# Attention scores in paired PSUM banks: row groups alternating, one mask product per bank

## The reference

```python
for l in range(DEPTH):                      # 2
    x = x + 0.5 * swiglu(rmsnorm(x), ...)   # D_FF = 2816
    c_q, c_kv, k_pe, q_s, k_s, v_s = split(rmsnorm(x) @ w_in[l])
    # latent group: 4 heads, 128 columns without and 64 with rotary, dense causal
    out_a = dense_causal_attention(q_a, k_a, v_a, MLA_QK ** -0.5)
    # window group: 8 heads of 64 over 2 key/value heads, window 128, a sink per head
    out_b = sliding_window_sink_attention(q_b, k_b, v_b, swa_sinks[l], SWA_HEAD_DIM ** -0.5)
    x = x + concat(rmsnorm(out_a), rmsnorm(out_b)) @ w_o[l]
    x = x + 0.5 * swiglu(rmsnorm(x), ...)
```

## Time and profile before

| | us |
|---|---|
| median of 3 runs | 1009.09 |
| lowest, highest | 1000.56, 1010.95 |
| span of the profiled execution, first to last instruction | 999.5 |
| own time of the profiled execution, taken as the run nearest above its span | 1000.56 |
| PE busy in it | 966.5 |
| DVE busy | 565.5 |
| ACT busy | 473.6 |
| attention of the first layer, block 0's scores to the fifth output chunk | 243.2 to 290.8 |

### The profile page before, as it was taken

The page is one execution under the profiler, slowest core; times in us unless marked ns, Lnnn a source line. Parts: engine busy times, 40 slices in busy tenths (PEclk is TensorE's granted clock), DMA queues, the critical chain, the costliest instruction groups (busy, mean ns, idle before and its releaser), DMA issues.

```text
span 999.5 us, 13783 instructions
## 1 busy us (share of the span) xinstructions
PE 966.5 (97%) x4504; PEld 773.4 (77%) x4504; DVE 565.5 (57%) x763; ACT 473.6 (47%) x831; POOL 53.0 (5%) x85
## 2 busy tenths in 40 slices
PE   5999999999899999999989999999998999999998
PEld 4888878888677878788768788887876777878876
DVE  4654545486766644545465454545877665454544
ACT  5543434464656544444355343435456654443433
POOL 2000000022110000000010000000220100000000
PEclk9999999999999999999989999999999999999999
DMA  8765554560044764646357555463501466464641
GB/s 296 248 198 181 174 203 155 182 212 21 22 158 142 232 226 132 227 146 212 124 184 230 192 170 208 153 222 129 190 1 59 156 206 230 138 222 147 208 170 43
DMA packets 46251, 168.61 MB, mean 169 GB/s; under 512 B 5216, under 2 KB 5216, under 8 KB 46208
## 3 DMA queue, kind: packets, MB, share of 16 engines
q1 hardware_dynamic: 44496, 162.02, 48.1%
q0 software_dynamic: 1568, 5.52, 1.8%
q10 hardware_dynamic: 144, 0.52, 0.1%
HBM read 167.00 MB, written 1.05 MB: 168 GB/s over the span
## 4 chain that ended last, share of the span: by engine, by line
issue 75%; PE 17%; POOL 5%; DMA 1%; DVE 1%; ACT 0%; POOLq 0%; DVEq 0%; ACTq 0%; SPq 0%
PE UV L919 3%; PE UV L917 3%; PE UV L918 3%; PE A L917 2%; PE A L918 2%; PE A L919 2%; POOL rs_x L307 1%; DMA raw<-stream 1%; POOL rs_s L307 1%; POOL rs_x L305 1%; POOL rs_m L307 1%; DVE xn L634 1%; POOL gain L285 0%; PE UV L961 0%; ACT whi L367 0%
## 5 line engine op out<-in xcount | busy, mean ns | idle before, releaser
L612 DVE TENSOR_TENSOR wlo<-raw,whi 128x1024 fp32r<-128x1024 f32 x306 | 361.8, 1222 | 113.2 <-ACT whi L367 112.9
L367 ACT ACTIVATE whi<-raw 128x1024 fp32r<-128x1024 f32 x306 | 308.0, 1053 | 114.7 <-DMA raw<-stream 113.8
L917 PE MATMUL UV<-whi,act_hi 128*128 128x512 f32 (+1 forms) x752 | 299.6, 398 | 4.1 <-issue 3.4
L919 PE MATMUL UV<-whi,act_lo 128*128 128x512 f32 (+1 forms) x752 | 292.2, 389 | 0.0
L918 PE MATMUL UV<-wlo,act_hi 128*128 128x512 f32 (+1 forms) x752 | 290.8, 387 | 0.0
L917 PEld LDWEIGHTS UV<-whi,act_hi 128*128 128x128 f32 x752 | 142.6, 190 | 32.7 <-issue 3.9
L919 PEld LDWEIGHTS UV<-whi,act_lo 128*128 128x128 f32 x752 | 142.3, 189 | 30.5
L918 PEld LDWEIGHTS UV<-wlo,act_hi 128*128 128x128 f32 x752 | 142.9, 190 | 27.3
L655 DVE TENSOR_TENSOR ht_lo<-UV,ht_hi 128x256 fp32r<-128x256 f32 x88 | 37.1, 422 | 213.4 <-ACT ht_hi L403 213.4
L403 ACT ACTIVATE ht_hi<-UV 128x256 fp32r<-128x256 f32 x88 | 33.2, 378 | 236.6 <-PE UV L961 236.6
L917 PE MATMUL A<-whi,ht_hi 128*128 128x512 f32 x352 | 141.7, 402 | 0.5 <-DVE ht_lo L655 0.4
(11 more groups left out here) (131 smaller groups left out, 655.3 us busy)
## 6 DMA issues: line engine op xcount, KB each, us to landing
raw<-stream SPq DMA_DIRECT2D x306, 512.0 KB, 4.4
gain<-norm_gains POOLq DMA_DIRECT2D x9, 512.0 KB, 5.7
out<-x SPq DMA_DIRECT2D x2, 512.0 KB, 2.6
sgain<-small_gains POOLq DMA_DIRECT2D x2, 324.0 KB, 5.0
x<-x_in SPq DMA_DIRECT2D x1, 512.0 KB, 3.4
x<-x_in ACTq DMA_DIRECT2D x1, 512.0 KB, 8.2
cs<-rope POOLq DMA_DIRECT2D x1, 128.0 KB, 6.0
cgain<-col_gains POOLq DMA_DIRECT2D x2, 1.0 KB, 5.5
```

The lines of the kernel that those rows point to most:

```text
L367: act.activation(whi_half(unit, half), raw[:, n % RAW, :], ACT.Copy).then_inc(hi_done, 1)
L612: dve.tensor_tensor(wlo_half(unit, half), raw[:, n % RAW, :], whi_half(unit, half).bitcast(F32), ALU.subtract).then_inc(split_done, 1)
L917: pe.matmul(dst, hi, w_hi, start=start, stop=False, skip_group_check=True)
L919: return pe.matmul(dst, lo, w_hi, start=False, stop=stop, skip_group_check=True)
```

## The change

The order of the window heads in `BANKS` changes, so that each even bank holds heads of the first key/value head (rows 0 to 63) and the next bank the matching heads of the second (rows 64 to 127). `scores` is gone. `latent_scores` forms both latent banks in one go: all four 128-row products, then the four 64-row products with the row group alternating from one to the next, then one mask product of two heads (256 columns) for each bank. `window_scores` forms two window banks in one go: one mask product of 512 columns for each, which starts the bank, then the heads' products with banks and row groups alternating. It waits for the exponentials of both banks before it. PE's order around them is rewritten by pairs. The orders of DVE, ACT, GpSimd and SP are as before.

```diff
         def score_banks(t):
             per = 4 // (t + 1)
-            return [(True, [0, 2]), (True, [1, 3])] + [(False, list(range(i, i + per))) for i in range(0, SH, per)]
+            swa = [(False, list(range(kv * 4 + i, kv * 4 + i + per))) for i in range(0, 4, per) for kv in range(SKV)]
+            return [(True, [0, 2]), (True, [1, 3])] + swa
...
+            def latent_scores(l, t):
+
+                wide = (t + 1) * P
+                for b in range(2):
+                    for j, hd in enumerate(BANKS[t][b][1]):
+                        pe.matmul(A[t][:, b, j * wide:(j + 1) * wide], qt[:, t, hd, :], kt[:, 2 + hd, 0:t + 1, :],
+                                  start=j == 0, stop=False, skip_group_check=True)
+                for j in range(2):
+                    for b in range(2):
+                        hd = BANKS[t][b][1][j]
                         r = ROPE * (hd % 2)
+                        pe.matmul(A[t][:, b, j * wide:(j + 1) * wide], qt[r:r + ROPE, t, 4 + hd // 2, :],
+                                  kt[r:r + ROPE, hd // 2, 0:t + 1, :], start=False, stop=False,
                                   skip_group_check=True)
+                for b in range(2):
+                    dst = heads(A[t][:, b, 0:2 * wide], 2)[:, :, t * P:wide]
+                    pe.matmul(dst, ident_b[:], over_heads(masks[:, 1, :], 2), start=False, stop=True,
+                              skip_group_check=True).then_inc(scores_done, 1)
+
+            def window_scores(l, t, b):
+
+                wide, per = (t + 1) * P, 4 // (t + 1)
+                pe.wait_ge(probs_ready, bank_no(l, t, b))
+                for i in range(2):
+                    mask = masks[:, 1 - t:2, :].rearrange("p a b -> p (a b)")
+                    masked = pe.matmul(A[t][:, i, :], ident_b[:], over_heads(mask, per), start=True, stop=False,
+                                       skip_group_check=True)
+                    first = masked if i == 0 else first
+                for j in range(per):
+                    for i in range(2):
+                        hd = BANKS[t][b + i][1][j]
+                        r = SD * i
+                        last = pe.matmul(A[t][:, i, j * wide:(j + 1) * wide], qt[r:r + SD, t, 6 + hd % 4, :],
+                                         kt[r:r + SD, 6, 0:t + 1, :], start=False, stop=j == per - 1,
                                          skip_group_check=True)
+                        if j == per - 1:
+                            last.then_inc(scores_done, 1)
                 return first
...
-                scores(l, 0, 0)
-                scores(l, 0, 1)
+                latent_scores(l, 0)
                 latent_products(l, 1)
                 transpose_probs(l, 0, 0)
-                scores(l, 0, 2).then_inc(unit_freed, 2)
                 values(l, 0, 0)
                 transpose_probs(l, 0, 1)
-                scores(l, 0, 3)
+                window_scores(l, 0, 2).then_inc(unit_freed, 2)
                 values(l, 0, 1)
...
+                latent_scores(l, 1)
+                transpose_probs(l, 1, 0)
+                transpose_norm(l, 2, 0)
+                values(l, 1, 0)
+                transpose_probs(l, 1, 1)
+                window_scores(l, 1, 2)
+                output_chunk(l, 0, 0)
+                values(l, 1, 1)
+                transpose_probs(l, 1, 2)
+                output_chunk(l, 0, 1)
+                values(l, 1, 2)
+                transpose_probs(l, 1, 3)
+                window_scores(l, 1, 4)
+                output_chunk(l, 0, 2)
+                values(l, 1, 3)
+                transpose_probs(l, 1, 4)
+                output_chunk(l, 0, 3)
+                values(l, 1, 4)
+                transpose_probs(l, 1, 5)
+                values(l, 1, 5)
```

More of the change, by code:

```diff
@@ L1092, in transpose_qk @@
                     last.then_inc(qk_psum, 1)
-            def scores(l, t, b):
-                latent_heads, hs = BANKS[t][b]
-                n, wide = bank_no(l, t, b), (t + 1) * P
-                if b >= 2:
-                    pe.wait_ge(probs_ready, n - 1)
-                for j, hd in enumerate(hs):
-                    dst = A[t][:, b % 2, j * wide:(j + 1) * wide]
-                    if latent_heads:
+            def latent_scores(l, t):
[7 more added lines that the diff above has]
+                        hd = BANKS[t][b][1][j]
@@ L1102, in scores @@
                         r = ROPE * (hd % 2)
-                        pe.matmul(dst, qt[:, t, hd, :], kt[:, 2 + hd, 0:t + 1, :], start=True, stop=False,
+                        pe.matmul(A[t][:, b, j * wide:(j + 1) * wide], qt[r:r + ROPE, t, 4 + hd // 2, :],
+                                  kt[r:r + ROPE, hd // 2, 0:t + 1, :], start=False, stop=False,
                                   skip_group_check=True)
-                        pe.matmul(dst, qt[r:r + ROPE, t, 4 + hd // 2, :], kt[r:r + ROPE, hd // 2, 0:t + 1, :],
-                                  start=False, stop=False, skip_group_check=True)
@@ L1107, in scores @@
-                        last = pe.matmul(dst[:, t * P:wide], ident_b[:], masks[:, 1, :], start=False, stop=True,
-                                         skip_group_check=True)
-                    else:
-                        r = SD * (hd // 4)
-                        pe.matmul(dst, qt[r:r + SD, t, 6 + hd % 4, :], kt[r:r + SD, 6, 0:t + 1, :], start=True,
-                                  stop=False, skip_group_check=True)
-                        last = pe.matmul(dst, ident_b[:], masks[:, 1 - t:2, :], start=False, stop=True,
-                                         skip_group_check=True)
@@ L1115, in scores @@
-                    first = last if j == 0 else first
-                last.then_inc(scores_done, 1)
+                for b in range(2):
[16 more added lines that the diff above has]
+                                         kt[r:r + SD, 6, 0:t + 1, :], start=False, stop=j == per - 1,
+                                         skip_group_check=True)
+                        if j == per - 1:
+                            last.then_inc(scores_done, 1)
@@ L1196, in _ @@
                 pe.wait_ge(qk_dve, l * TB + 2)
-                scores(l, 1, 0)
-                scores(l, 1, 1)
-                k = 0
-                for b in range(len(BANKS[1])):
-                    transpose_probs(l, 1, b)
-                    if b + 2 < len(BANKS[1]):
-                        scores(l, 1, b + 2)
-                    if b == 0:
-                        transpose_norm(l, 2, 0)
-                    elif b != 3:
-                        output_chunk(l, 0, k)
-                        k += 1
-                    values(l, 1, b)
+                latent_scores(l, 1)
[18 more added lines that the diff above has]
+                values(l, 1, 5)
                 for k in range(4, KD - 1):
```

## The result

| | before | after |
|---|---|---|
| median, 20 runs of each | 1003.68 | 1008.88 |
| lowest, highest | 999.44, 1010.95 | 1004.37, 1012.71 |
| span of the profiled execution | 999.5 | 1005.9 |
| ratio after/before, 95% interval | | 1.0042, 1.0023 to 1.0062 |

The changed kernel is slower. The ratio gives 0.42%, 4.2 us, and its interval leaves no change out; the medians lie 5.2 us apart. The times of the kernel before fall in two groups, 12 of them at 999.4 to 1003.8 and 8 at 1007.5 to 1011.0 us; what sets them apart is looked at in the last experiments. The changed kernel's median stands 7.2 us above that of the lower group, 1001.7.

A forecast was written before the change was run, and what follows sets the result against it. TensorE was taken to bound the kernel. Removed work against block 1's new waits gave +5.6 us serial or +1.6 overlapped for two layers; the middle, +3.6, on the median 1009.09 gave 1012.7 us, range 1003 to 1023.

The forecast's parts named there:

- Score blocks: New latent and window blocks on PE: 6.2 us of work removed per layer, up to 3.0 more if row groups overlap.
- the middle that I took: Whole kernel: +3.6 us, between +5.6 with row groups serial and +1.6 with them overlapped.
- rival D: Score blocks: alternation overlaps nothing, the serial end, 1014.7 us; inside the forecast's 0.62.
- rival B: Score blocks: each turn between row groups costs 0.2 us, +12.5 in all, 1021.6 us; chance 0.06.
- its check by removed work: Block 1, serial: 6.0 us of new waits against 2.9 of work removed, +3.1.
- my overlapped end: Whole kernel with passes of the two row groups side by side: +1.6 us for two layers.
- Block 0: Of 3.3 us PE work removed there, 0.3 to 1.1 come through by DVE's chain; the rest becomes PE idle.
- Block 1's waits: PE waits 2.2 us for exponentials, 1.1 for norm, 1.6 to 2.0 before first output chunk, 0.86 for last copy.
- Rival C: Block 1: the waits don't come and removed work comes through, -12.4 to -18.4 us, 991 to 997; chance 0.12.
- rival A: The clock falls in block 1's new waits in both layers, 3.1 us each, +9.8, 1018.9 us; chance 0.20.
- one of my own signs of being wrong: Changed kernel's trace: the granted clock shows a second fall.
- The base: Whole kernel: the +3.6 us was added to the median of three times, 1009.09, giving 1012.7.

The follow-up runs named there:

- the last experiments: Useless bf16 products put into PE's waits: the kernel before 1001.29 us (0.9972), grouped 994.27 us (0.9911), and nlfirst_warm 999.94 us (0.9964).
- warm: Changed kernel with useless bf16 products put into four of PE's waits in a layer: 1002.62 us, ratio to before 0.9995.
- b0only: Changed kernel with block 1 put back as before, pairs kept in block 0 only: 999.77 us, ratio to before 0.9968.
- nlfirst_warm: warm with DVE's low part of activations ahead of bank 2's maxima, two more fills, none before the first output chunk: 999.94 us, ratio to before 0.9964.
- latsplit_nl: Changed kernel with DVE's low part ahead of bank 2's maxima and block 1's latent banks formed one after the other: 1001.26 us, ratio to before 0.9942.
- grouped: Kernel before, one bank at a time, with products inside each bank regrouped by row count and one mask product: 996.06 us, ratio to before 0.9920.
- b1only: Changed kernel with block 0 put back as before, pairs kept in block 1 only: 1011.49 us, ratio to before 1.0083.

## Why the prediction was right and wrong

**Score blocks: right at the lower end, wrong in the middle that I took.** I gave 2.3, 4.0 and 2.4 us serial or 2.0, 3.4 and 1.7 to 1.8 overlapped. Measured: 1.85 (244.95 to 246.80) and 3.34 for the latent blocks, 1.68, 1.66 and 1.59 for the window pairs. No row of before had two row groups side by side, and I took the middle between the ends. That step failed, by 1.0 us a layer: overlap is full, one pass more in each block than the one a turn that I counted, and rival D (no overlap) and rival B (a turn costs 0.2 us) are both false. I also priced block 1's eight old window heads at 6.7 us; from 270.33, 274.35, 278.73 and 283.08 they took 1.59, 1.51, 1.51 and 1.60, 6.2 together. The forecast of the stage doesn't rest on it, but its check by removed work came out at the same +3.1 partly by luck. With the clock held the change would be +0.9 us (2 x 0.45), below my overlapped end of +1.6.

**Block 0: right, at its upper end.** I let 0.3 to 1.1 of the removed work come through, by DVE's chain; at full clock it is 1.16 a layer (warm), in b0only 1.1.

**Block 1's waits: right, each within 0.25 us.** 1.98, 1.08, 2.01 and 0.69 for 2.2, 1.1, 1.6 to 2.0 and 0.86. At full clock block 1 takes 27.76, +1.6, where the overlapped end of the stage was +1.9. nlfirst_warm shows the third wait's cause and value, latsplit_nl that of the first: its block 1 is 0.8 us shorter still than nlfirst_warm's at a share of 1.00. Rival C, that the waits don't come, is false; but latsplit_nl and grouped show that they belong to the pairing and to DVE's order, and not to grouped products.

**The clock: the step that failed.** The forecast put the clock at nothing; rival A, that it falls in the new waits, had 0.20. It fell in all four parts, and a second fall in the trace was one of my own signs of being wrong. What spoke for holding was the stretch from 257 to 264, with PE busy 4.00 of 7 us at 1.00. That was one execution. b1only ran the same stretch in its second layer and lost the clock right behind it, and 24 of 89 runs of before lie in the upper group, a group that 12 of 12 runs with fills in this stretch didn't show. So the row was no evidence that emptier stretches are safe. I also priced the fall too high: 3.1 for block 1 and about 1 for block 0, taken from 6 us at 0.55 where PE was never idle. Measured by warm it is 1.07 and 0.78 in the profiled execution, since the stretch in block 1 was 3.4 us long and the one in block 0 lay partly over idle time. The size is not fixed: b1only's second layer lost 33.23 - 27.76 = 5.5 us, with about 14 us at the lower level (2 x 0.21 x 33.23), a part of them due to the old waits. And the profiled execution is one of the lighter ones: its mean clock is 0.988, and the 20 runs have 0.981 to 0.990.

**The sum: near in size by luck.** +3.6 was predicted and +4.2 measured. The prediction had +1.8 a layer with the clock held, where warm shows +0.45, 1.35 too much, most of it by the middle of the overlap; and it left out the clock's 1.85. 2 x (0.45 + 1.85) = +4.6 is the profiled attention's +4.7, as it must be, for 0.45 and 1.85 are differences of the same stretches. And the +4.2 is small because 8 of the 20 runs of before had lost some of the clock themselves. Against the lower group, to which the profile behind the forecast belongs, the change is +7.2, twice what I predicted; of the 2.5 us beyond the profiled attention, no profile shows where they lie.

**What can be told from no change: wrong.** I said hardly less than 1%. With 20 runs of each the interval is 0.2% to either side, so +0.4% is a real slowdown.

**The base.** The time given, 1012.7, was 3.6 above a median of three, 1009.09, of which two lay in the upper group. The 20 runs have 1003.68, and I had noted the 8.5 us without a reason. The runs of before in the later sets point to it: a mean clock of 0.986 to 0.992 in the upper group where the lower one has 0.994 to 1.000. For the first three runs no clock is on record.

## What to carry to other kernels

Work taken off the busiest engine is worth its time only where the order keeps that engine covered: the same regrouping gained 1.4 us a layer in block 1 with one bank in flight over the other, and lost 1.6 with two banks closed together. With the latent banks taken apart again and one line moved on DVE, block 1 took 0.3 less than before although its window banks stayed paired. Before closing two banks at once, write down for each consumer engine what then stands in front of the next thing PE needs, and move it (here one line on DVE, 1.1 us a layer). Every new wait of PE of 1 to 2 us should be priced with a fall of the clock too, and a single profile at full clock is no proof that it holds: look at the clocks of all runs, and at whether the times fall in two groups.

## What the runs showed of the hardware that was not expected

- The clock fell to 1.2 GHz behind waits of 1.9 to 2.0 us (block 0: 1.88, then 0.69; block 1: 1.98, then 1.08 with 0.66 us of work between them). In the changed kernel it stayed there for 6.8 and 3.4 us. In b1only's second layer it fell behind block 0's old waits of 1.15 and 1.41 us. The Trainium skill, TensorE: Matmul & The Clock Gate, section HAM oscillation, ties such falls to idle gaps between bursts, in an example with waits of about 3 to 5 us; the traces agree on the tie, and PE's waits in this attention are about 2 us at most. A few us of bf16 products whose output is overwritten took the falls away in nlfirst_warm altogether.
- A fall costs what it covers: nothing in block 0 of b0only (20.37 us at 0.83) and of grouped's second layer (19.50 at 0.91), 1.1 us in grouped's first (20.57 at 0.83), 0.8 and 1.1 us a block in the changed kernel, 5.5 in b1only.
- Two row groups of 64 rows overlap fully in f32, two passes and all, even when up to four passes of one group stand in the program ahead of those of the other (1.14 us in either order). With sixteen passes, eight of each group, the order matters: 1.71 against 1.16 us.
